# Two layers of a hybrid backbone on one core: token-row mLSTM, column groups, and new orders in six stages

## Time and profile before

| | |
|---|---|
| median of 3 runs | 2545.69 us (2539.39 to 2553.2) |
| the profiled execution | 2536.03 us, of it span from first to last instruction 2533.1 us |
| busy in the span | PE 2113.0, DVE 998.8, ACT 692.0, POOL 330.1 us |
| mean granted TensorE clock | 0.897 of full speed |
| read from memory | 634 MB, 261 GB/s over the span |

### The profile page before, as it was taken

One profiled execution on the slowest core, in us unless ns is written; L12 is line 12 of the kernel. 1 busy time (PEld: TensorE's weight loads), 2 busy tenths in 40 slices (PEclk: granted clock), 3 DMA queues, 4 the chain that ended last, 5 costly groups with the idle time before them and its releaser, 6 DMA issues. The chain is left out here.

```text
span 2533.1 us, 58768 instructions
## 1 busy us (share of the span) xinstructions
PE 2113.0 (83%) x26249; PEld 1422.0 (56%) x26249; DVE 998.8 (39%) x1629; ACT 692.0 (27%) x1482; POOL 330.1 (13%) x208
## 2 busy tenths in 40 slices
PE   6999999788898978988678779678888888977775
PEld 2777755433675444544343478378778856743343
DVE  2283237566314111111233377466667662311113
ACT  3134522355322000001031332446444421100001
POOL 0333300000230000000100054131311100000000
PEclk8999988898897988989889889799999988888788
DMA  8363520500435589877820030000000023799984
GB/s 277 119 235 137 195 100 1 200 1 1 133 103 205 205 308 339 290 261 276 309 97 34 1 125 26 1 4 4 4 4 4 4 77 128 267 367 346 346 320 165
DMA packets 180962, 381.07 MB, mean 150 GB/s; under 512 B 11242, under 2 KB 40518, under 8 KB 180454
## 3 DMA queue, kind: packets, MB, share of 16 engines
q1 hardware_dynamic: 162160, 343.74, 38.1%
q10 hardware_dynamic: 15094, 20.99, 2.7%
q0 software_dynamic: 3456, 12.58, 1.4%
HBM read 634.46 MB, written 25.95 MB: 261 GB/s over the span
## 5 line engine op out<-in xcount | busy, mean ns | idle before, releaser
L1726 PE MATMUL banks<-arena 128*32 128x256 f32 x1696 | 238.4, 431 | 95.0 <-DMA arena<-in_exp_w_up_dram 94.7
L368 PE MATMUL banks<-parts 128*128 128x512 f32 (+1 forms) x1096 | 242.9, 374 | 23.9 <-DVE parts L382 20.7
L1727 PE MATMUL banks<-arena 128*32 128x256 f32 x1696 | 238.4, 431 | 0.0
L368 PEld LDWEIGHTS banks<-parts 128*128 128x128 f32 x1096 | 194.7, 192 | 60.8 <-DVE parts L382 11.5
L1726 PEld LDWEIGHTS banks<-arena 128*32 128x32 f32 x1696 | 107.3, 122 | 186.6 <-DMA arena<-in_exp_w_up_dram 103.0
L2411 PE MATMUL banks<-arena 64*64 64x64 f32 x4224 | 159.8, 226 | 47.9 <-DVE arena L379 20.0
L376 DVE TENSOR_TENSOR arena<-banks,arena 64x256 f32<-64x256 f32 (+3 forms) x128 | 65.4, 511 | 330.1 <-ACT arena L1790 252.2
L1790 ACT ACTIVATE arena<-banks 64x256 f32<-64x256 f32 x78 | 29.7, 380 | 571.8 <-PE banks L1727 571.8
L2411 PEld LDWEIGHTS banks<-arena 64*64 64x64 f32 x4224 | 148.1, 141 | 53.3 <-DVE arena L379 21.4
L368 PE MATMUL banks<-arena,ring 128*128 128x256 f32 (+2 forms) x544 | 162.8, 461 | 8.6 <-PEq L315 8.6
L2411 PE MATMUL banks<-ring 64*64 64x64 f32 x4224 | 160.0, 225 | 7.9 <-issue 7.7
(11 more groups left out here) (349 smaller groups left out, 3730.3 us busy)
## 6 DMA issues: line engine op xcount, KB each, us to landing
arena<-in_exp_w_gate_dram SPq DMA_DIRECT2D x106, 1024.0 KB
arena<-in_exp_w_up_dram SPq DMA_DIRECT2D x106, 1024.0 KB
arena<-in_exp_w_down_dram SPq DMA_DIRECT2D x53, 2048.0 KB
ring<-in_exp_w_gate_dram SPq DMA_DIRECT2D x50, 1024.0 KB
ring<-in_exp_w_up_dram SPq DMA_DIRECT2D x50, 1024.0 KB
ring<-in_exp_w_down_dram SPq DMA_DIRECT2D x25, 2048.0 KB
ring<-in_w_mod_dram SPq DMA_DIRECT2D x24, 2048.0 KB, 9.2
ring<-in_ab_w_in_dram SPq DMA_DIRECT2D x10, 2048.0 KB, 13.6
```

Source lines behind the costliest of these rows:

```text
L368: m = nc.tensor.matmul(o, a, b, start=first and n == 0, stop=last and n == len(pairs) - 1)
L1726: nc.tensor.matmul(o[r:r + BLOCK, 0:256], x, up[:, k, c], start=k == 0, stop=k == KD - 1)
L1727: m = nc.tensor.matmul(o[64 + r:64 + r + BLOCK, 0:256], x, gate[:, k, c], start=k == 0, stop=k == KD - 1)
```

## The change

- *Gates:* the three products go to partitions 0 to 7, 32 to 39 and 64 to 95 of one bank, interleaved over k. u's low part for tile k is made once tile k was used. h's save is issued ahead of one ring piece.
- *mLSTM:* numerators come token-major: for each of four tiles of 128 tokens, weights `a_e` (128 keys x 128 tokens) and moving values of 257 columns, the last of them ones, so that column 256 is the denominator. exp(-m) is turned to columns in the block before. The reciprocal is of 128 x 1; direction 0 is scaled by ACT on its way out of the bank, direction 1 added by DVE; ACT squares and sums each head's row. Banks 5 to 7 are used in turn.
- *Its norm:* three pieces of modulation first; then rows are scaled by 128 x 1 inverses, turned by PE, and weighted and gated in one pass.
- *Scan:* y of a pair is read after the next iteration's weights.
- *Its norm and the output projection:* the first 8 mixed rows are split in the norm; the norm's room moves and has 8 tiles.
- *Experts:* logit parts with 32 weights columns (16 are zero) in four groups over k, moving 512 (256) tokens, copied, and added over quarters with a small matrix after two turned tiles. ACT copies all turned tokens. In layer 0 positions come before the second shared tile, in layer 1 before the first.
- *Last rows:* in layer 1, h's latent rows and the gain are turned to token-major between expert blocks; the end is computed in token rows and stored in four parts; `write_out` goes.
- *MLA projection:* plain and swapped rotated key rows go to groups 64 to 95 and 96 to 127, interleaved. *Heads:* weights of a head have 128 columns, 96 of them plain and 32 swapped, so one product serves both; two heads' keys go to two groups of 64, interleaved.
- *Attention:* jobs go two heads at one query tile; exponential, maximum and scores run one to two jobs ahead; the outputs of two heads go to two groups of 64, interleaved, and are read later.

```diff
@@ modulation @@
+    stream_weights(piece_at[("x", 2)] - NSLOT)
+    nc.sync.dma_start(h_saved, h[:]).then_inc(h_saved_done, 16)
     stream_weights(piece_at[("mod", 0, 3)])
-    nc.sync.dma_start(h_saved, h[:]).then_inc(h_saved_done, 16)
@@ project_gates @@
-    w = weights("gates")
-    for i in range(2):
-        mms(bank("pg", i)[0:8, :], [(w[:, k, 8 * i:8 * i + 8], a_u_plain[:, k, :]) for k in range(8)]).then_inc(pe_done, pe.tick(("pg", i), *((let_go("gates"),) if i == 1 else ())))
-    w = weights(("x", 2))
-    mms(bank("pg", 2)[0:32, :], [(w[:, k, 256:288], a_u_plain[:, k, :]) for k in range(8)]).then_inc(pe_done, pe.tick(("pg", 2)))
+    w, w_dt = weights("gates"), weights(("x", 2))
+    for k in range(KD):
+        for rows, x in ((slice(0, 8), w[:, k, 0:8]), (slice(32, 40), w[:, k, 8:16]), (slice(64, 96), w_dt[:, k, 256:288])):
+            m = nc.tensor.matmul(ps[0][rows, :], x, a_u_plain[:, k, :], start=k == 0, stop=k == KD - 1)
+        m.then_inc(pe_done, pe.tick(("u used", k), *((("pg", 0), let_go("gates")) if k == KD - 1 else ())))
...
-    for j in range(13):
-        if j == 3:
-            for k in range(KD):
-                dve.wait_ge(*at(("u high", k)))
-                vsub(u_low[:, k, :], a_u_plain[:, k, :], whole(u_high[:, k, :])).then_inc(dve_done, dve.tick(("u low", k)))
...
+    for k in range(KD):
+        dve.wait_ge(*at(("u high", k)))
+        dve.wait_ge(*at(("u used", k)))
+        vsub(u_low[:, k, :], a_u_plain[:, k, :], whole(u_high[:, k, :])).then_inc(dve_done, dve.tick(("u low", k)))
@@ mlstm @@
-        for s in range(TT):
-            pe.wait_ge(*at(("E", it, s)))
...
-        nc.tensor.matmul(ps[3], selector(it), a_em[:, d], start=True, stop=True).then_inc(pe_done, pe.tick(("em", it)))
         if it + 1 < n:
...
-        for k, (s, spans) in enumerate(SPAN[d]):
-            pe.wait_ge(*at(("sD", it, s)))
-            for half in range(3):
-                w = ones[:] if half == 2 else a_v[:, s, hd * MLV + half * P:hd * MLV + half * P + P]
-                for i, (c0, c1) in enumerate(spans):
-                    m = nc.tensor.matmul(ps[5 + half][:, c0:c1], w, a_e[:, it % 2, s, c0:c1], start=k == 0,
-                                         stop=k == TT - 1 and i == len(spans) - 1)
-        m.then_inc(pe_done, pe.tick(("num", it)))
+        for i, t in enumerate(tile_order[d]):
+            pe.wait_ge(*at(("tile out", 4 * it + i - 3)))
+            of = sources(d, t)
+            for k, s in enumerate(of):
+                pe.wait_ge(*at(("sD", it, s)))
+                m = nc.tensor.matmul(tile_bank(it, i)[:, 0:MLV + 1], a_e[:, it % 2, s, t * P:(t + 1) * P], a_v[:, s, hd, :],
+                                     start=k == 0, stop=k == len(of) - 1)
+            m.then_inc(pe_done, pe.tick(("num", it, i)))
...
+        for i, t in enumerate(tile_order[d]):
+            if it + 1 < n:
+                exponentials_row(it + 1, i)
+            at_ = 4 * it + i
+            if d == 0:
+                act.wait_ge(*at(("inv", at_)))
+                nc.scalar.activation(token_tile(it, t), tile_bank(it, i)[:, 0:MLV], ACT.Copy, scale=head_inv[:, at_:at_ + 1]).then_inc(
+                    act_done, act.tick(("tile out", at_)))
+            else:
+                act.wait_ge(*at(("tile out", at_)))
+                act.wait_ge(*at(("head square", TT * hd + i - 2)))
+                nc.scalar.activation(scratch[:, 256 * (i % 2):256 * (i % 2) + MLV], token_tile(it, t), ACT.Square,
+                                     accum_out=head_sums[:, TT * hd + t:TT * hd + t + 1]).then_inc(
+                    act_done, act.tick(("head square", TT * hd + i)))
...
+        dve.wait_ge(*at(("num", it, i)))
+        inv, den = head_inv[:, at_:at_ + 1], tile_bank(it, i)[:, MLV:MLV + 1]
+        dve.step(nc.vector.tensor_tensor(inv, c_em[:, d, t, d * MLH + hd:d * MLH + hd + 1], den, ALU.max))
+        dve.step(nc.vector.scalar_tensor_tensor(inv, den, -1.0, inv, ALU.mult, ALU.max))
+        dve.step(nc.vector.reciprocal(inv, inv), ("inv", at_))
+        if d == 1:
+            o = token_tile(it, t)
+            dve.wait_ge(*at(("tile out", 4 * (it - 1) + t)))
+            nc.vector.scalar_tensor_tensor(o, tile_bank(it, i)[:, 0:MLV], inv, o, ALU.mult, ALU.add).then_inc(
+                dve_done, dve.tick(("tile out", at_)))
...
-        if it > 0:
-            finish(it - 1)
-        if it + 1 < n:
-            weights_of(it + 1)
...
+        for i in range(TT):
+            finish_tile(it, i)
+            if more and i > 0:
+                weights_row(it + 1, i - 1)
+        if more:
+            weights_row(it + 1, TT - 1)
@@ mlstm_out @@
+    beside.pe_first(3)
     for k in range(8):
-        pe.wait_ge(*at(("hsq", k)))
-        for q in range(4):
-            m = nc.tensor.matmul(ps[4][32 * q:32 * q + 32, P * (k // 2):P * (k // 2) + P], ones[:, 0:32],
-                                 sq[:, k, P * q:P * q + P], start=k % 2 == 0, stop=k % 2 == 1)
-    m.then_inc(pe_done, pe.tick("hsums"))
-    beside.pe_first(3)
-    pe.wait_ge(*at("hinv"))
-    for hd in range(MLH):
-        for q in range(4):
-            m = nc.tensor.matmul(ps[hd][:, P * q:P * q + P], row_of(32 * q), root[:, P * hd:P * hd + P], start=True, stop=True)
-        m.then_inc(pe_done, pe.tick(("hspread", hd)))
+        if k % 2 == 0:
+            for j in range(2 * k, 2 * k + 4):
+                pe.wait_ge(*at(("normed", j)))
+        if k >= 5:
+            pe.wait_ge(*at(("gated", k - 5)))
+        for t in range(TT):
+            m = nc.tensor.transpose(ps[k % 5][:, t * P:(t + 1) * P], a_h[:, t, k * P:(k + 1) * P], ident[:])
+        m.then_inc(pe_done, pe.tick(("h turned", k)))
@@ ssd @@
+        if it % 4 == 0 and it > 0:
+            read_pair(p - 1)
+    read_pair(n // 4 - 1)
+
+def read_pair(p):
+    dve.wait_ge(*at(("y", 4 * p + 3)))
+    x = xs(p, 0, T)
@@ ssd_norm @@
+    beside.pe_first(2)
     for k in range(8):
...
+    for k in range(4):
+        split_mix_low(k)
     norm.invert()
@@ moe_block @@
-    for t in range(nt):
-        c = slice(c0 + t * P, c0 + t * P + P)
-        mms(ps[0][:, t * NE:(t + 1) * NE], [(m_v[:, k, c], m_rw[:, k, :]) for k in range(KD)]).then_inc(pe_done, pe.tick("logits"))
+    for k in range(KD):
+        q = 32 * (k % 4)
+        m = nc.tensor.matmul(ps[0][q:q + 32, 0:n], m_rw[:, k, :], m_v[:, k, c0:T], start=k < 4, stop=k >= 4)
+    m.then_inc(pe_done, pe.tick("logit parts"))
     for j in range(2 * nt):
+        if j == 2:
+            pe.wait_ge(*at("parts out"))
+            for t in range(nt):
+                m = nc.tensor.matmul(ps[7][:, t * NE:(t + 1) * NE], m_logit_parts[:, t * P:(t + 1) * P], quarters, start=True, stop=True)
+            m.then_inc(pe_done, pe.tick("logits"))
...
+    if l == 1:
+        positions()
...
+        if f == 0 and l == 0:
             positions()
...
+        vmul(o[:, t, 0, :], m_ysh[:, t, :], m_gain).then_inc(dve_done, dve.tick(("y gained", t)))
+        dve.wait_ge(*at(("y root", t)))
+        dve.step(nc.vector.reciprocal(roots[:, t:t + 1], roots[:, t:t + 1]), ("y gained", t))
+        for half in range(2):
+            c = slice(512 * half, 512 * half + 512)
+            one(o[:, t, 0, c], o[:, t, 0, c], roots[:, t:t + 1], m_htok[:, t, c], ALU.mult, ALU.add).then_inc(
+                dve_done, dve.tick(("out", t, half)))
@@ project_mla @@
-    mms(ps[5][64:96, :], [(w[:, k, 256:288], b_u[:, k, :]) for k in range(KD)])
     pe.wait_ge(*at("kr swapped"))
-    mms(ps[6][64:96, :], [(n_krs[:, k, :], b_u[:, k, :]) for k in range(KD)]).then_inc(pe_done, pe.tick("kr", let_go("mkv")))
+    for k in range(KD):
+        nc.tensor.matmul(ps[5][64:96, :], w[:, k, 256:288], b_u[:, k, :], start=k == 0, stop=k == KD - 1)
+        m = nc.tensor.matmul(ps[5][96:128, :], n_krs[:, k, :], b_u[:, k, :], start=k == 0, stop=k == KD - 1)
+    m.then_inc(pe_done, pe.tick("kr", let_go("mkv")))
@@ attention_heads @@
+            mms(ps[hd % 4][:, 0:NL], [(n_uq[:, k, hd, :], n_q[:, k, :]) for k in range(3)]).then_inc(pe_done, pe.tick(("q", hd)))
+        pe.wait_ge(*at(("k read", 2 * pair - 4)))
+        pe.wait_ge(*at(("k read", 2 * pair - 3)))
+        for k in range(2):
+            for i in range(2):
+                m = nc.tensor.matmul(ps[4 + pair % 2][64 * i:64 * i + 64, :], ukv[:, k, 2 * pair + i, 0:64], n_kv[:, k, :],
+                                     start=k == 0, stop=k == 1)
+        m.then_inc(pe_done, pe.tick(("k", pair)))
...
-        mms(o[0:HD, 0:NL], [(n_uq[:, k, hd * HD:(hd + 1) * HD], n_q[:, k, :]) for k in range(3)])
-        mms(o[r, NL:T], [(n_uqs[:, k, hd * ROPE:(hd + 1) * ROPE], n_q[:, k, :]) for k in range(3)]).then_inc(pe_done, pe.tick(("ah", 2 * hd)))
-        mms(bank("ah", 2 * hd + 1)[0:64, :], [(ukv[:, k, hd, 0:64], n_kv[:, k, :]) for k in range(2)]).then_inc(pe_done, pe.tick(("ah", 2 * hd + 1)))
@@ attention @@
-            pe.wait_ge(*at(("att read", hd // 2 - 2)))
-        rows = slice(64 * (hd % 2), 64 * (hd % 2) + 64)
```

(18 more changed lines are left out.)

457 lines of the change are left out of this document (247 added, 210 removed).

## The result

2371.5 us (median of 4 runs, 2369.1 to 2381.8) beside 2545.8 for the kernel before (4 runs, 2539.4 to 2553.2): ratio 0.934, 95% interval 0.931 to 0.938. The profiled execution took 2371.3 us, span 2369.5, so 163.6 less span than before, where the prediction took 159 off. The forecast for the median was 2387, in a range of 2360 to 2405.

A forecast was written before the change was run, and what follows sets the result against it. PE was taken as the bound, busy 2113 of 2533 us, with holes lowering its clock in mLSTM, scan and attention. Stage terms summed to -159 us, so 2545.7 became 2387 us, range 2360 to 2405 (2358 to 2425 with rivals).

The forecast's parts named there:

- First split job: Gates: job 0 takes the 5.6 us of its neighbours instead of 8.5, saving 2.9 us.
- The gates' sum: Gates: 24 matmuls in 8.5 us saves 13.7, an earlier low part of u saves 2.9, together -16.5 us.
- hand-offs: mLSTM: waits that three banks don't cover, 0.5 us a direction, 4 us in all.
- tile-chain rival: mLSTM: PE, three VectorE steps, ScalarE copy and bank release bound it; 88 us instead of 68, total 2410; chance 14%.
- start and dips: State-space scan: start 5, end 1.5 and a clock dip or two 2 us, on top of 107 us.
- The norm's 4 us: mLSTM's norm: sums start at once, 3.8 us earlier, and each streamed piece lands that much earlier; -4 us.
- Loads did not swallow it: Layer 0's experts: rival that loads swallow the router's gain of 9 us; +9, total 2396; chance 11%.
- one job ahead, PE needs 1280 columns, 2.14 us: Attention: 16 jobs at 2.14 us are 34, plus start 4, end 3, dips 3: 44 us, -24.
- The bound of -14 for an exposed softmax: Attention: gain of only 14 us instead of 24 if every second job still exposes its softmax.
- groups do overlap: Heads, attention, gates, MLA, router: rival that column groups don't overlap; +38 us, total 2425; chance 6%.
- stayed low: mLSTM, scan, attention, heads: rival that they run at 1.2 GHz throughout; about +217 us, total 2604; chance 3%.
- the median of the runs is 9.7 above it: Whole kernel: runs' median taken 9.7 us above the profiled execution's 2536.0, so 2545.7 less 159 gives 2387 us.

The follow-up runs named there:

- the paired scan: Changed kernel with both heads of a state-space scan pair done side by side, in alternating 64-row groups: scan 104.4 us for 111.7, total 2371.2 us.
- the scan run: Changed kernel with the state-space scan's read of y put back ahead of the next weights: scan 137.8 us, total 2406.7 us.

## Why the prediction was right, and where it was not

- **Gates, MLA, heads, output projection:** each within 1.3 us. That pairs of 64 overlap, for which no row of before stood, shows in 1.94 against 3.65 us and in the paired scan. First split job: PE starts it at 52.67 and its successor at 58.36, 5.7 for 5.6. The output projection's first product starts 3.9 us into its block (554.39). The gates' sum is better than its parts: the 24 matmuls took 9.74 us, not 8.5, because the first six passes of each product lay at the lower clock, 0.86 us each, where in the kernel before it was four (at the upper one three load in each 0.43 us, a full overlap); and the nine later jobs took 49.6 us instead of 51.3, at a clock of 1.00 instead of 0.97, which nobody had forecast.
- **mLSTM:** right mechanism, term too small by 7. PE is busy for 55.4 us, what I had (58 less 3); but I added 4 for hand-offs, 7 for the start and 2 for the end, and all three together are 5.4. PE begins 0.8 us after the block's start and the first tile at 6.2, busy for 4.9 of them. PE's matmuls never wait for tile copies; taking the third bank away costs 7.7, so the tile-chain rival was wrong in place and, at 88, in price. How the 56 us divide among fewer columns, the reciprocal that went and the clock (0.83 to 1.00) no run separates: PE is busy for 44 us less and stands still for 12 us less.
- **Scan:** right, shown by putting the read back (137.8). 4 better than the sum because start and dips, put at 8.5, took less. VectorE waits for y once, 1.5 us, at the end of the stage, where the forecast had no wait over 0.5.
- **The norm's 4 us:** what failed is the 3.8 us by which the first sums were to let go of their piece earlier, and that the work behind the last piece would take as long as before. The first let-go came 1.7 us earlier relative to the block (the next load is issued at 382.51 after 378.2, before at 459.32 after 453.3), since the first sums were slower; the step after it held, the last piece came 1.9 earlier; and the end at the lower clock took 2.5 back. In the scan run, where first and last sums are at the upper clock, the load is issued 3.2 us earlier and the stage is 3.3 us shorter. So the mechanism is there, at most 3.3 of the 4 us, and in the profiles at 0.79 the clock takes it all.
- **Layer 0's experts:** PE reaches the shared expert 10.9 us earlier (8.8 us after the block's start, 684.45, against 19.7), for 9. The loop itself wanders in unchanged code between 489 and 497 us in twelve profiles (median 492), so 11 is the reading, and the 14 of this profile is partly luck; the kernel before has one profile, which may have wandered as far. Loads did not swallow it. **Layer 1:** -7.3 for -8. Its load issue comes 40.5 us into the block, before 41.5, unmoved but for 1 us; that one microsecond can't be told from the wander, the rest is the end.
- **Attention:** the step that failed is "one job ahead, PE needs 1280 columns, 2.14 us", with 16 x 2.14 as the sum. I added up each engine's work and took the largest, and never walked the lists against each other: VectorE's list has the maximum of j + 1, which needs scores queued behind turn j - 1, ahead of the division that turn j waits for. That loop is 2.9 us. At 52.5 us the stage met the prediction's own sign of being wrong, attention over 50. The bound of -14 for an exposed softmax was the right number for a reason I hadn't named. With two lines swapped a job takes 2.13 us, the price that the sum had, and the forecast's 44 is beaten, at 38.8, because start, end and dips, put at 10, take under 5.
- **The rivals:** groups do overlap, loads don't swallow the gain, the clock rose (0.897 to 0.913) rather than stayed low. The total of 159 for 164 hides +8 in attention, +5 in the norm, -7, -4 and -5 elsewhere: the sum was better than its terms, which is luck.
- **2387 for 2371.5:** of these 15.5 us, 5.8 are the terms' (164.8 between the profiled executions, for 159). The other 9.7 are the step "the median of the runs is 9.7 above it". The profiled execution of the kernel before was faster than all its timed runs, that of the kernel after is the median of its own, so the 9.7 did not carry over. The range of 2360 to 2405 held it.

What stays open: what picks the clock's course in the norm, and how much of the paired scan's 104 to 107 us is VectorE and how much PE at the lower level.

## What to carry to other kernels

Before you price a software pipeline by its busiest engine, walk once round it: from each wait to what stands ahead of it in the other engine's list; a step placed one line too early closed a loop that cost 14 us, and more buffers didn't open it. Products that fill half or a quarter of the output partitions go side by side in column groups, and a read-back belongs behind the next round's work. Compare a stage with its own repeats in runs that don't touch it before crediting 4 us to an edit.
